# The next block's first output section ahead of the final norm, with its residual input loaded into the gated products' tiles

## What is computed

```python
h = rmsnorm(x, norm_mix_g); u = h @ w_in                    # 1024 -> 2828 columns
mix = concat(rglru(u), ssd(u), gated_delta(u), s5(u))       # four mixers, 256 columns each, recurrent over tokens
x = x + mix @ w_out
x = x + cross_attend(rmsnorm(x, norm_cross_g), mem_k, mem_v, w_cq, w_co)   # 4 heads, 256 memory tokens
x = x + (silu(h2 @ w_gate) * (h2 @ w_up)) @ w_down          # h2 = rmsnorm(x, norm_ffn_g), 2816 hidden
y = rmsnorm(x, norm_final_g)
```

## Time and profile before

| what | value |
|---|---|
| time, median of 3 runs (lowest to highest) | 3831.66 us (3827.7 to 3832.4) |
| the profiled execution's own time | 3830.37 us |
| its span, first to last instruction | 3828.6 us |
| mean granted TensorE clock | 0.965 |
| busy: TensorE, VectorE, ScalarE, GpSimd | 91%, 56%, 34%, 2% |
| mean share of the 16 DMA engines, rate | about 60%, 206 GB/s |
| loads of a mixer chunk (page's list of DMAs) | 384, 384, 256, 256 and 128 KB |

### The profile page before, as it was taken

The page is one execution under the profiler, slowest core; times in us unless marked ns, Lnnn a source line. Parts: engine busy times, 40 slices in busy tenths (PEclk is TensorE's granted clock), DMA queues, the critical chain, the costliest instruction groups (busy, mean ns, idle before and its releaser), DMA issues.

```text
span 3828.6 us, 61402 instructions
## 1 busy us (share of the span) xinstructions
PE 3483.1 (91%) x23786; PEld 3100.4 (81%) x23786; DVE 2145.7 (56%) x4395; ACT 1290.8 (34%) x2325; POOL 89.9 (2%) x288
## 2 busy tenths in 40 slices
PE   6778888978899888999999899999988999989998
PEld 5766667866888878788888787888788899989998
DVE  5647756464776755655667345444573655644223
ACT  5454344241544434332333233122233331223001
POOL 1210000000000000000000000000000000000000
PEclk9998899989999999999999999999999999999999
DMA  5665554658555475555656744545568555576776
GB/s 190 210 224 205 182 172 157 210 188 262 188 184 191 165 263 187 197 208 196 232 218 220 277 146 160 179 171 186 172 214 294 191 202 194 203 254 228 248 251 214
DMA packets 329090, 787.83 MB, mean 206 GB/s; under 512 B 29920, under 2 KB 148576, under 8 KB 328416
## 3 DMA queue, kind: packets, MB, share of 16 engines
q1 hardware_dynamic: 301984, 748.90, 56.9%
q10 hardware_dynamic: 26816, 35.01, 2.5%
HBM read 609.22 MB, written 174.57 MB: 205 GB/s over the span
## 4 chain that ended last, share of the span: by engine, by line
issue 52%; PE 37%; DVE 4%; ACT 2%; POOLq 2%; DVEq 1%; DMA 1%; ACTq 1%; POOL 0%; SPq 0%
PE banks L480 11%; PE banks L482 11%; PE banks L481 11%; PE banks L1703 1%; DMA wlo_sb<-kept_dram 1%; ACT whi_sb L961 0%; PE banks L1673 0%; DVEq L1274 0%; DVE hl_sb L1235 0%; DVE uc_sb L1310 0%; POOLq L2211 0%; POOLq L2209 0%; PE banks L1683 0%; DVE m_p_sb L2278 0%; DVE rstd_sb L1378 0%
## 5 line engine op out<-in xcount | busy, mean ns | idle before, releaser
L480 PE MATMUL banks<-hh_sb,whi_sb 128*128 128x384 f32 (+1 forms) x2800 | 1057.0, 377 | 94.7 <-DVE hl_sb L1235 30.5
L481 PE MATMUL banks<-hh_sb,wlo_sb 128*128 128x384 f32 (+1 forms) x2800 | 1025.4, 366 | 0.0
L482 PE MATMUL banks<-hl_sb,whi_sb 128*128 128x384 f32 (+1 forms) x2800 | 1024.0, 366 | 0.0
L480 PEld LDWEIGHTS banks<-hh_sb,whi_sb 128*128 128x128 f32 x2800 | 542.1, 194 | 164.9 <-issue 38.2
L482 PEld LDWEIGHTS banks<-hl_sb,whi_sb 128*128 128x128 f32 x2800 | 540.7, 193 | 50.6
L481 PEld LDWEIGHTS banks<-hh_sb,wlo_sb 128*128 128x128 f32 x2800 | 543.1, 194 | 45.7 <-issue 0.7
L480 PE MATMUL banks<-g_hi_sb,whi_sb 128*128 128x384 f32 (+2 forms) x1264 | 458.8, 363 | 29.9 <-DVE x_sb L1424 15.1
L482 PE MATMUL banks<-g_lo_sb,whi_sb 128*128 128x384 f32 (+2 forms) x1264 | 446.8, 353 | 0.0
L481 PE MATMUL banks<-g_hi_sb,wlo_sb 128*128 128x384 f32 (+2 forms) x1264 | 446.5, 353 | 0.0
L1424 DVE TENSOR_TENSOR x_sb<-x_sb,banks 128x384 f32<-128x384 f32 (+3 forms) x336 | 193.8, 584 | 284.8 <-PE banks L482 266.6
L1216 DVE TENSOR_TENSOR wlo_sb<-raw_sb,whi_sb 128x1024 fp32r<-128x1024 f32 x203 | 248.2, 1226 | 149.2 <-ACT whi_sb L961 145.3
(11 more groups left out here) (445 smaller groups left out, 4705.4 us busy)
## 6 DMA issues: line engine op xcount, KB each, us to landing
whi_sb<-kept_dram SPq DMA_DIRECT2D x392, 512.0 KB, 3.7
wlo_sb<-kept_dram SPq DMA_DIRECT2D x392, 512.0 KB, 4.8
raw_sb<-w SPq DMA_DIRECT2D x176, 512.0 KB, 4.8
kept_dram<-whi_sb SPq DMA_DIRECT2D x112, 512.0 KB, 5.1
kept_dram<-wlo_sb SPq DMA_DIRECT2D x112, 512.0 KB, 6.0
uc_dram<-uc_sb ACTq DMA_DIRECT2D x54, 192.0 KB, 3.2
uc_dram<-uc_sb ACTq DMA_DIRECT2D x36, 256.0 KB, 2.0
plain_sb<-w SPq DMA_DIRECT2D x32, 256.0 KB, 4.9
```

The costliest lines, as they stand in the source:

```text
L480: eng.matmul(out, xh, yh, start=first, stop=False)
L481: eng.matmul(out, xl, yh, start=False, stop=False)
L482: return eng.matmul(out, xh, yl, start=False, stop=last)
```

## The change

At the two places where block follows block (`RESIDUAL` holds their passes, 1 and 4):

- The section list is now: last four `d`, w0, `st`, four `final`, w1. `stage_b` gets the held-back list as `end` and inserts it behind w0. w0's square moves to w1.
- SP loads x for the new pass into `g_free`, as soon as all fills before w0 are done (`sp_residual`), and no longer waits for stores there. VectorE adds `g_free` and the bank into `x`.
- The add of w0 is not made at its own section but at the end of the last `final` section, behind the eight scalings. It waits for x in `g_free` and for both stores of x[0] and x[1]; w2, w4 and w6 wait for their pair's stores.
- The stores of these two final norms are issued by ScalarE (`store_final`) and not by SP.
- The mixer's window of block 1 starts at the same section number, behind which `st` and `final` now lie.

```diff
-    def stage_b(p, hy):
+    def stage_b(p, hy, end):
...
+        if end:
+            out[1].squares = out[0].squares + out[1].squares
+            out[0].squares = []
+            out[1:1] = end
...
+        if end:
+            residual[p] = early
+            early += 1
...
-            a = [st] + end
+            end = [st] + end
         secs += a
+        if a:
+            end = []
         if p + 1 < NP:
-            windows.append((p + 1, first, len(secs) - (2 if secs[-1].kind == "z" else 11)))
+            windows.append((p + 1, first, len(secs) - (2 if secs[-1].kind == "z" else 6)))
+    secs += end
...
+            elif s.kind == "final" and s.p + 1 in RESIDUAL:      # ScalarE
+                store_final(eng, s)
...
+        def dve_add(eng, s):
+            n, out = cols(s.p), x[:, s.a, 0:cols(s.p)]
+            dve_preps(eng, before_adds(s))
+            bank = bank_in(eng, s.f)
+            if s.p in RESIDUAL:
+                if s.a == 0:
+                    eng.wait_ge(y_loaded, 64 * RESIDUAL[s.p] + 64)
+                if s.a % 2 == 0:
+                    eng.wait_ge(out_stored[s.a // 2], 32 * s.p)
+                before = g_free[:, s.a // 4, s.a % 4, 0:n]
+            else:
...
+            eng.tensor_tensor(out, before, bank[:, 0:n], ALU.add).then_inc(x_done, 1)
+            eng.drain().then_inc(free[s.f % 3], 1)
...
+                if s.a or s.p not in RESIDUAL:                   # at a w section
+                    dve_add(eng, s)
...
+                if s.a == KD - 2 and s.p + 1 in RESIDUAL:        # at the last final section
+                    dve_add(eng, next(o for o in SECS if o.kind == "w" and o.p == s.p + 1))
...
+        def store_final(eng, s):
+            t0, n = PASSES[s.p][0] * P, cols(s.p)
+            for k in (s.a, s.a + 1):
+                eng.wait_ge(out_ready, KD * s.p + k + 1)
+                eng.dma_start(t["y_t"][:, k, t0:t0 + n], x[:, k, 0:n]).then_inc(out_stored[k // 2], 16)
...
+        def sp_residual(eng, i):
+            eng.wait_ge(full, SECS[i].f)
+            p = SECS[i].p
+            t0, n = PASSES[p][0] * P, cols(p)
+            for q in range(KD // 2):
+                eng.dma_start(g_free[:, q // 2, q % 2 * 2:q % 2 * 2 + 2, 0:n],
+                              t["x_t"][:, 2 * q:2 * q + 2, t0:t0 + n]).then_inc(y_loaded, 16)
```

More of the change, by code:

```diff
@@ L257, in schedule @@
     early = 0
+    residual, end = {}, []
     for p in range(NP):
+        if end:
+            residual[p] = early
+            early += 1
         hy = new_h("Y", p)
@@ L269, in schedule @@
         first = len(secs)
-        b = stage_b(p, hy)
+        b = stage_b(p, hy, end)
         secs += b
-        last = [secs[-4 + i] for i in range(4)]
+        last = [s for s in b if s.kind == "d"][-4:]
         if 0 < p < NP - 2:
@@ L356, in schedule @@
         s.after = w
-    return secs, hs, ns, uses, w_fill, fills_of_h, windows
-SECS, HS, NS, USES, W_FILL, H_FILLS, WINDOWS = schedule()
+    return secs, hs, ns, uses, w_fill, fills_of_h, windows, residual
+SECS, HS, NS, USES, W_FILL, H_FILLS, WINDOWS, RESIDUAL = schedule()
 N_W = len(USES)
@@ L1367, in dve_second @@
                 dve_norm_tail(eng, SECS[i])
+        def dve_add(eng, s):
[9 more added lines that the diff above has]
+            else:
+                if s.a == 0:
+                    eng.wait_ge(x_loaded, 64 * sum(p not in RESIDUAL for p in range(s.p + 1)))
+                before = out
+            eng.tensor_tensor(out, before, bank[:, 0:n], ALU.add).then_inc(x_done, 1)
+            eng.drain().then_inc(free[s.f % 3], 1)
         def dve_section(eng, i):
@@ L1394, in dve_section @@
             elif s.kind == "w":
[L1395 to L1400, removed]
+                if s.a or s.p not in RESIDUAL:
+                    dve_add(eng, s)
             elif scores_at(i) is not None:
@@ L1587, in sp_section @@
             elif s.kind == "w" and s.a == 0:
-                for q in range(KD // 2 if s.p in (0, 1, NP - 1) else 0):
-                    sp_x(eng, s.p, q)
+                if s.p in RESIDUAL:
+                    sp_residual(eng, i)
                 if s.p == 0:
+                    for q in range(KD // 2):
+                        sp_x(eng, 0, q)
                     for slot in range(UCS):
@@ L1602, in sp_section @@
                     sp_cache(eng, k)
[L1603 to L1606, removed]
+            elif s.kind == "final" and s.p + 1 not in RESIDUAL:
+                store_final(eng, s)
         per_chunk = dict(
```

## The result

The changed kernel is slower: median 3833.28 us (12 runs) against 3827.5 of before (12 runs), ratio 1.0018, interval 1.0009 to 1.0026. (The three runs shown ahead of the prediction had their median at 3831.66, high among the twelve.) In a second set of runs it was 1.0012 (1.0003 to 1.0021). The forecast was 6.0 us less; by the ratio it is 6.9 us more: the other direction, though under the 0.2% that was taken as no change. The median lies inside the stated range of 3819 to 3834, but that is luck: the range stood on a before of 3831.7, and on the 3827.5 of the twelve runs it would have been 3815 to 3830.

A forecast was written before the change was run, and what follows sets the result against it. TensorE, busy 91%, was taken as the bound, with time won only where it idles. The two places' 4.2 + 2.6 = 6.8 us, less 0.8 for the mixer, gave 6.0: 3831.7 to 3825.7 us, range 3819 to 3834.

The forecast's parts named there:

- (d): Both places: landing of the first pair of stores that w0's add waits for, taken as 4.0 us, between 1.9 and 10.4.
- (e): Block 1's mixer sections, spread from w1 instead of w2 on: -0.8 us taken, with ends of -3.5 and +5.
- (a): w0 ahead of the statistics: scalings about 0.95 us later at place one, 1.5 at place two, whose 2.07 idle goes.
- (b): x loads early into free tiles, w2's weights issued near 1390.5: TensorE's waits of 6.82, 5.34 and 1.60 us lose their cause.
- (c): New TensorE wait before w2: later of scalings' end and first pair's landing, plus the add (0.69 or 0.56 us) and 0.05.
- R2: New wait dearer than the old: first pair lands at 10.4 us behind 7 MB of loads; 3838.5 us; chance 0.14.
- R3: Mixer's shift dominates, places as forecast: 3.5 us lost (3828.4) or 5 won (3819.9); chance 0.17, half each way.

The follow-up runs named there:

- e4: The changed kernel with the first two scaled tiles stored from the load slots, so w0's add waits for no store; 0.9989 of before, 3825.32 us.
- e2: The kernel before with only block 1's mixer sections spread from w1 on, as in the changed kernel; 1.0016 of before, 6.1 us slower.
- e7: The changed kernel with the final norms' stores issued by the SP queue and the mixer spread as before the change; 0.9967 of before, 3816.84 us.
- e3: The changed kernel with the stores of the two final norms issued by the SP queue again; 0.9989 of before, 3825.05 us.
- e12: e6 with the changed kernel's spread of the mixer and nothing else changed; 0.9982 of before, 3820.1 us.
- e6: The changed kernel with the old order (statistics and finals ahead of w0) and the mixer spread as before; 0.9962 of before, 3815.53 us.
- e1: The changed kernel with the mixer's sections spread as before the change; 1.0011 of before.
- e13: The changed kernel measured again, with nothing altered; 1.0012 of before.
- e9: The changed kernel, stores still by ScalarE, but the SP queue stands at the final sections until each pair is scaled; 0.9983 of before, 3825.37 us.

## Why the prediction was wrong

The two terms that failed in size are (d), the landing of the stores, and (e), the mixer's plan; (a) was off by less. By the prediction's steps:

- **(a)** Place two came as forecast: w0 runs without a wait and the scalings start 8.1 us behind the down-projection's end (8.11 forecast). At place one the scalings start 19.4 us behind that end, not 17.3. Three things are in it. First, w0's weights, issued at 1384.97, were not there near 1391: the wait of 7.04 is for their load. w0 so began about where it began before (7.04 against 7.36 us behind the end). Second, it ran slower: TensorE, idle for those 7 us, was granted 0.50, the lower level of 1.2 GHz, over the first 3.8 us, where before the whole of w0 had 0.84 (1394.1 to 1400.7). It ended 1.3 us later than before. The low parts, which I took for the limit, were ready first (1398.66, and TensorE came to them at 1400.35). Third, a row was misread: 1399.83 is not the last start of w0 in the kernel before. A section is 24 matmuls; three more follow, and w0 ended at 1400.8, 0.7 us behind the 1400.1 that the sum used. The first 3.8 us of w0 in the changed kernel, with the columns of the earlier trace rows:

```profile
1393.50:1397.30 3.80, 3.80 (x9) 3.03 (x10) 0.00 (x0) 0.63 (x1) 0.00 (x0) 0.50 0.84 325
```

- **(b)** w2's weights were to be issued near 1390.5. They were at 1396.09, since SP waited 6.2 us for the landing of the kept copy in that weight slot. That was still soon enough, so the step held where it mattered: there is no wait for weights before w2, and the 1.60 before w3 is gone.
- **(c)** The new wait was named rightly, and e4 shows it: w2 starts behind the later of the scalings and the first pair's landing, plus the add.
- **(d) is the first term that failed in size.** 4.0 us were taken, 7.2 and 7.9 measured. By the prediction's own formula (14.0 minus twice the landing is what the places win) the 6.0 us won become 1.1 lost, 7.1 us in all. With the 2 us of (a), w2 comes 5.4 and 4.1 us later than forecast, and by w4 the two places have lost 1.5 us where 6.8 were to be won. The bounds held it (1.9 to 10.4); the choice inside went by queue and size. But ScalarE's medians of 3.2 and 5.4 are over the whole span, with the DMA engines full at some of these stores and not at others. The trace of the kernel before could have sorted them: from 721 to 745, with the DMA engines at a share of 1.02, the eight stores of z (128 KB, ScalarE's queue) took 6.1 us at the median, and from 488 to 513, at a share of 0.35, eight took 1.7. The prediction had added up 7 MB of loads around the stores and foreseen a backlog, and then took the 4.0 from rows that do not tell whether there was one. The row of 721 to 745:

```profile
z_dram<-uc_sb ACTq DMA_DIRECT2D x8, 128.0 KB, 6.1
```

- **(e) is the other.** -0.8 was taken, about 6 measured: e2 1.0016; e7 against e3 22 ten-thousandths; e12 against e6, from two sets of runs, 20. The same comparison in the changed kernel (e1) gives only 7, or 1 against its second measurement, within the intervals. The mechanism, the fifth section in front of the low parts, was counted through rightly: the first scores start 3.7 us later behind w6 than before (19.2 against 15.6), where 3.5 was counted. It was then averaged against 5 us of relief. The relief did not come: the 2.33 wait at 1473.46 has become one of 2.70 on ScalarE behind it. What stays open is the way from there to 6. No one wait holds it; single profiles place 2 to 10 us there by block 2 and 3 to 8 by the last statistics. The mean granted clock was 0.9617 in the runs of e2 and of e13, 0.9631 in those of before beside them. Within before's own runs 0.001 of it goes with 1.7 to 2.1 us, so by an estimate from these figures 2 to 3 us come with the clock. Whether the longer waits lower it, or something else does, is not shown.
- **The rivals.** R2 (slower, the price of the landing), at a smaller landing than its 10.4, and the bad half of R3 are what happened, together. The table gives 1.5 us for the places and e2 6.1 for the mixer: 7.6 against 6.9 and 4.6 measured. That they meet so nearly is within the noise. R2 and R3 had been priced mostly apart, and their sum was given too little of the chance.

As for the Trainium skill's round-robin between queues (DMA: Bandwidth & Descriptors, "Queues, rings and completion order"), the trace agrees for a part of the time only. Here are three windows of the changed kernel, 1407 to 1410, 1410 to 1414 and 1414 to 1418, with packets, MB and share of 16 engines. q1 is SP's queue; q10 is ScalarE's, whose first store was issued at 1406.48:

```profile
q1 hardware_dynamic: 349, 1.24, 101.9%
q10 hardware_dynamic: 6, 0.01, 0.8%
```

```profile
q1 hardware_dynamic: 335, 1.17, 71.9%
q10 hardware_dynamic: 334, 0.46, 31.1%
```

```profile
q10 hardware_dynamic: 748, 1.02, 68.8%
q1 hardware_dynamic: 789, 0.50, 39.1%
```

Once both queues have packets running they move equally many (335 and 334), as packet-by-packet turns would. But up to 3.5 us behind the issue ScalarE's queue had moved 6 packets, 0.01 MB: its store had hardly started. And equal packets were not equal bytes: 0.46 MB went to the store's queue against 1.17. Half of the rate from the start would have given about 4 us, an estimate (384 KB at half of some 400 GB/s, and the 1.9 of the quiet landing). It lacked the delay ahead of the start, and the half was 28%.

## What to carry to other kernels

When a wait moves from a load to a store, read the store's landing in a stretch with as many loads beside it as the freed queue will issue, and not from the queue's median over the whole span.

A reorder that puts one more section ahead of a release costs a buffer. Here w0 ahead of the finals took the bank that would have hidden the landing. The same change without the reorder, with the mixer's plan held, is 0.4% faster than before instead of 0.2% slower.

A planner that spreads work by position answers to every inserted section. Hold its plan fixed while judging the edit.

## What was not expected of the hardware

- A store from another queue than the one that was full of loads hardly started for 3 to 3.5 us. In e9, with SP standing still, ScalarE's queue moved 0.23 MB between 0.5 and 1.5 us behind its first issue (1409.46). At the median the same 192 KB landed in 2.7 us there and in 8.4 in the changed kernel.
- Issue itself can take long. The timeline of the SP queue in the changed kernel has two loads of the mixer whose issue took 6.01 and 2.93 us, against 0.76 and 2.02 at the same two in the kernel before, and medians of 0.37 and 0.47 over the 17 times that each is issued. The DMA share was 1.00 there and 1.01 at those of before, so full engines alone do not explain it; what does is not shown.

```profile
1403.38 6.01 SPq L2870 DMA_DIRECT2D m_in_l_sb<-uc_dram  x1
1409.43 2.93 SPq L2871 DMA_DIRECT2D m_in_l_sb<-uc_dram  x1
```
